# Five norms ahead of projections: one product with equal weights, a square root on ScalarE, a reciprocal on VectorE

## The reference

```python
def rms_norm(x, g):      # first block
    y = xf * lax.rsqrt(jnp.mean(xf * xf, axis=-1, keepdims=True) + EPS)
    return y * g

def layer_norm(x, g, b): # second block
    var = jnp.mean(jnp.square(xf - mu), -1, keepdims=True)
    return (xf - mu) * lax.rsqrt(var + LN_EPS) * g + b

# first block
proj = rms_norm(x, g_mix_pre) @ w_in          # place A
...
x = x + rms_norm(y, g_mix_post)
h = rms_norm(x, g_ffn_pre)                     # place B
x = x + rms_norm(conv_ffn(h, w_up, ..., w_down), g_ffn_post)
...
# second block, layers 0 and 1
x = layer_norm(ALPHA * x + y, ln_mix_g, ln_mix_b)                     # C (layer 0), E (layer 1)
x = layer_norm(ALPHA * x + swiglu(x, w_gate, w_up, w_down), ...)      # D (layer 0), read by od_w_in
```

## Time and profile before

| | |
|---|---|
| median of 3 runs | 914.29 us (914.2 to 915.26) |
| profiled execution | 914.49 us |
| its span in the profile | 912.7 us |
| PE busy | 890.2 us, 98% |
| PE weight loads | 843.1 us, 92% |
| DVE busy | 675.0 us, 74% |
| ACT busy | 507.9 us, 56% |
| POOL busy | 121.6 us, 13% |
| mean granted TensorE clock | 0.996 |

### The profile page before, as it was taken

One profiled execution on the slowest core, in us unless ns is written; L12 is line 12 of the kernel. 1 busy time (PEld: TensorE's weight loads), 2 busy tenths in 40 slices (PEclk: granted clock), 3 DMA queues, 4 the chain that ended last, 5 costly groups with the idle time before them and its releaser, 6 DMA issues.

```text
span 912.7 us, 18172 instructions
## 1 busy us (share of the span) xinstructions
PE 890.2 (98%) x6780; PEld 843.1 (92%) x6780; DVE 675.0 (74%) x1113; ACT 507.9 (56%) x750; POOL 121.6 (13%) x78
## 2 busy tenths in 40 slices
PE   5999899999999999999999999999999999999997
PEld 5977899999999999889999999999889999999996
DVE  5975797777777866788766686788767887668665
ACT  6345644334335645967555555566387765555552
POOL 1000000000000023002133230300130023324003
PEclk9999999999999999999999999999999999999999
DMA  8853275555564655445655655543334475555531
GB/s 311 324 212 116 70 225 189 184 188 179 184 196 151 198 193 163 139 140 161 208 173 174 198 175 178 164 128 126 116 117 139 126 229 187 173 195 176 180 139 46
DMA packets 44147, 156.76 MB, mean 172 GB/s; under 512 B 5082, under 2 KB 5573, under 8 KB 43973
## 3 DMA queue, kind: packets, MB, share of 16 engines
q1 hardware_dynamic: 42336, 152.17, 51.1%
q10 hardware_dynamic: 1317, 2.36, 0.7%
q0 software_dynamic: 448, 1.59, 0.5%
HBM read 155.04 MB, written 1.06 MB: 171 GB/s over the span
## 4 chain that ended last, share of the span: by engine, by line
PE 91%; ACT 3%; DVE 3%; issue 1%; DMA 1%; POOL 0%; SPq 0%; DVEq 0%; POOLq 0%
PE ps L399 21%; PE ps L400 21%; PE ps L401 21%; PE ps L444 5%; PE ps L446 5%; PE ps L445 5%; PE ps L416 2%; PE ps L423 1%; PE ps L417 1%; PE ps L793 1%; PE ps L504 1%; PE ps L506 1%; PE ps L505 1%; PE ps L528 1%; PE ps L814 1%
## 5 line engine op out<-in xcount | busy, mean ns | idle before, releaser
L399 PE MATMUL ps<-op_hi,w_hi 128*128 128x258 f32 (+1 forms) x1322 | 375.2, 284 | 1.6 <-DVE op_lo L1482 1.6
L401 PE MATMUL ps<-op_hi,w_lo 128*128 128x258 f32 (+1 forms) x1322 | 372.7, 282 | 0.0
L400 PE MATMUL ps<-op_lo,w_hi 128*128 128x258 f32 (+1 forms) x1322 | 372.4, 282 | 0.0
L1329 DVE TENSOR_TENSOR w_lo<-raw,w_hi 128x1024 fp32r<-128x1024 f32 x224 | 289.2, 1317 | 22.2 <-ACT w_hi L977 19.5
L977 ACT ACTIVATE w_hi<-raw 128x1024 fp32r<-128x1024 f32 x224 | 231.6, 1053 | 75.3 <-PE ps L401 41.7
L399 PEld LDWEIGHTS ps<-op_hi,w_hi 128*128 128x128 f32 x1322 | 249.6, 189 | 5.0 <-ACT bias L1289 2.0
L400 PEld LDWEIGHTS ps<-op_lo,w_hi 128*128 128x128 f32 x1322 | 250.4, 189 | 2.0
L401 PEld LDWEIGHTS ps<-op_hi,w_lo 128*128 128x128 f32 x1322 | 249.4, 189 | 0.0
L972 ACT ACTIVATE w_hi<-raw 128x1024 fp32r<-128x1024 f32 x60 | 63.5, 1058 | 61.7 <-PE ps L401 31.3
L399 PE MATMUL ps<-mix_hi,w_hi 128*128 128x256 f32 x336 | 96.0, 286 | 0.0
L400 PE MATMUL ps<-mix_lo,w_hi 128*128 128x256 f32 x336 | 94.6, 281 | 0.0
(11 more groups left out here) (278 smaller groups left out, 1081.8 us busy)
## 6 DMA issues: line engine op xcount, KB each, us to landing
raw<-in_stream SPq DMA_DIRECT2D x284, 512.0 KB, 3.6
x<-in_x SPq DMA_DIRECT2D x4, 256.0 KB, 5.7
bias<-bias_rows POOLq DMA_DIRECT2D x1, 1024.0 KB, 8.0
work<-in_last_norm SPq DMA_DIRECT2D x1, 1024.0 KB, 5.6
result<-y SPq DMA_DIRECT2D x4, 256.0 KB, 2.0
spans<-in_spans ACTq DMA_DIRECT2D x1, 576.0 KB
bias<-bias_rows POOLq DMA_DIRECT2D x1, 512.0 KB, 10.7
proj<-in_gmask ACTq DMA_DIRECT2D x1, 512.0 KB
```

The lines of the kernel that those rows point to most:

```text
L399: pe.matmul(o, wh, xh, start=start, stop=False, **kw)
L400: pe.matmul(o, wh, xl, start=False, stop=False, **kw)
L401: return pe.matmul(o, wl, xh, start=False, stop=stop, **kw)
L1329: m = dve.tensor_tensor(w_lo[:, s, :], raw[:, s, :], fp(w_hi[:, s, :]), ALU.subtract)
```

## The change

The mean square is now computed so that it comes out on all partitions at once, as a row of 256 tokens: one matmul with the 128 x 128 tile of 1/1024 as weights and the summed squares as the moving operand. ACT takes the square root from PSUM, with eps as its bias, and DVE the reciprocal.

- `sum_squares` adds down to one chunk: two additions of 512 columns as before, a third of 512, one of 256. PE's only wait is for the last.
- `square_mean` is one matmul of 256 columns. In the three networks it stands behind the first half of the third hidden unit's product, where it stood ahead of it.
- `spread` at A to E, the eps addition and POOL's power there are gone, and with them DVE's wait for POOL ahead of `split_lo`. POOL's list of statistics falls from seven to three (one at A, two elsewhere in the last layer).
- ACT gets `load_root` behind the squares (a Sqrt of one column that is used for nothing, so that the table set is loaded there), and `take_root` behind the next `split_hi`. At A, `load_root` first waits for two small memsets of POOL.
- DVE: `invert_root` (a `reciprocal` of 256 columns) in place of `copy_rinv`. At D it stands ahead of the `step()` that it followed.
- At A and B, PE computes the mean by token as well, from the one summed chunk (two matmuls of one column, four in the profile). At B, DVE makes `tok_ffn` from it right behind the reciprocal, ahead of the first hidden chunk; before it stood behind it.

The core of the diff:

```diff
-        STATISTICS = (2, 2, 2, 2, 4, 8, 2)
+        STATISTICS = (2, 4, 8)
...
             def square_mean(b):
-                def src(c):
-                    if c % 4 == 0:
-                        sums[0] += 1
-                        pe.wait_ge(S["sq_summed"], sums[0])
-                    return sq[:, c, :]
-                token_means(b, [(0, 0, [lambda c=c: src(c) for c in (0, 1, 4)])])
+                sums[0] += 1
+                pe.wait_ge(S["sq_summed"], sums[0])
+                pe.matmul(chunk(b, 0), mean_w[:, 0, :], sq[:, 0, :], start=True, stop=True, skip_group_check=True
+                          ).then_inc(S["square_mean_done"], 1)
...
                 first_chunks(bank(4, 0, n), bank(5, 0, n), operand, hi, lo)
+                out_chunk(bank(6, 0, n), hi, lo, half=0)
                 pe.wait_ge(S[free[0]], free[1])
                 square_mean(0)
-                out_chunk(bank(6, 0, n), hi, lo, half=0)
-                spread([(0, 0, SEQ), (1, 0, SEQ + P)])
+                if not shifted:
+                    token_means(1, [(0, 0, [sq[:, 0, :]])])
                 out_chunk(bank(6, 0, n), hi, lo, half=1)
...
                 if c == 0:
                     pe.wait_ge(S["pool_const"], 4)
                     square_mean(6)
+                    token_means(5, [(0, 0, [sq[:, 0, :]])])
                     pe.wait_ge(S["consts_loaded"], 16 * len(consts))
                     pe.matmul(ps[0:HEADS, 7, 0:384], rel[:], strip, start=True, stop=True
                               ).then_inc(S["table_ready"], 1)
-                if c == 2:
-                    spread([(0, 6, SEQ), (1, 6, SEQ + P)])
...
                 if c == 2:
-                    out_chunk(bank(2, 0, SEQ + 2), *raw_operand, half=0)
-                    spread([(0, 6, SEQ), (1, 6, SEQ + P)])
-                    out_chunk(bank(2, 0, SEQ + 2), *raw_operand, half=1)
+                    out_chunk(bank(2, 0, SEQ + 2), *raw_operand)
...
+            def load_root():
+                act.activation(root_warm[:], eps_col[:, 0:1], ACT.Sqrt)
+
+            def take_root(b, eps):
+                roots[0] += 1
+                act.wait_ge(S["square_mean_done"], roots[0])
+                act.activation(rinv[:, SEQ:512], chunk(b, 0), ACT.Sqrt, bias=eps_col[:, eps:eps + 1]
+                               ).then_inc(S["std_ready"], 1)
...
                     for part in range(2):
                         step(ahead=not (late and isinstance(j, int) and j == NFF - 1))
+                        if part == 0 and isinstance(j, int) and j == 0:
+                            take_root(0, 0 if convolve else 1)
...
-                m = dve.tensor_tensor(pair(sq, i), pair(sq, i), pair(sq, i + 1), ALU.add)
+                own.done(dve.tensor_tensor(pair(sq, i), pair(sq, i), pair(sq, i + 1), ALU.add))
                 if half:
-                    chained(m)
-                    m = dve.tensor_tensor(sq[:, 4, :], sq[:, 4, :], sq[:, 5, :], ALU.add)
-                m.then_inc(S["sq_summed"], 1)
+                    own.settle()
+                    chained(dve.tensor_tensor(pair(sq, 0), pair(sq, 0), pair(sq, 2), ALU.add))
+                    dve.tensor_tensor(sq[:, 0, :], sq[:, 0, :], sq[:, 1, :], ALU.add).then_inc(S["sq_summed"], 1)
...
-            def copy_rinv(b):
+            def invert_root():
                 rinvs[0] += 1
-                dve.wait_ge(S["spread_done"], stats.n)
-                dve.tensor_copy(rinv[:, 0:SEQ], chunk(b, 1)).then_inc(S["rinv_copied"], 1)
+                dve.wait_ge(S["std_ready"], rinvs[0] + 1)
+                dve.reciprocal(rinv[:, 0:SEQ], rinv[:, SEQ:512]).then_inc(S["rinv_copied"], 1)
                 dve.wait_ge(S["rinv_copied"], rinvs[0])
...
                     if begins:
-                        eps = RMS_EPS if convolve else LN_EPS
-                        hand_statistic(0, eps)
-                        dve.wait_ge(S["tok_rinv_ready"], stats.n)
                         step()
-                        copy_rinv(0)
+                        invert_root()
+                        if convolve:
+                            dve.wait_ge(S["stat_done"], 2)
+                            dve.tensor_scalar(tok_ffn[:], bank(1, 0, 2), RMS_EPS, RMS_EPS, ALU.add, ALU.mult)
...
                 if c == 0:
-                    hand_statistic(6, LN_EPS)
-                    dve.wait_ge(S["tok_rinv_ready"], stats.n)
-                step()
-                if c == 0:
-                    copy_rinv(6)
+                    invert_root()
+                step()
```

More of the change, by code:

```diff
@@ L136, in build @@
         minus_half = sb("minus_half", [P, 8])
+        eps_col = sb("eps_col", [P, 2])
+        root_warm = sb("root_warm", [P, 1])
         bias = sb("bias", [P, HEADS, 384])
@@ L192, in build @@
             split_hi_done split_done units_done sq_ready sq_summed mean_done
-            stat_done var_ready tok_rinv_ready spread_done x_ready norm_hi operand_ready z_ready centred evac
+            stat_done square_mean_done std_ready var_ready tok_rinv_ready spread_done x_ready norm_hi operand_ready z_ready centred evac
             row_sq_ready row_var_ready alpha_ready last_loaded row_root_ready rows_dve rows_act rows_turned
@@ L311, in _ @@
             pool.memset(minus_half[:], -0.5).then_inc(S["pool_const"], 1)
+            pool.memset(eps_col[:, 0:1], RMS_EPS).then_inc(S["pool_const"], 1)
+            pool.memset(eps_col[:, 1:2], LN_EPS).then_inc(S["pool_const"], 1)
             pool.memset(pad_b[:, :, 0:16], 0.0).then_inc(S["pool_const"], 1)
@@ L362, in _ @@
             row_roots(0)
-            inverse_root(1)
             row_roots(1)
@@ L371, in _ @@
             pool.memset(faded[0], 0.0).then_inc(S["faded_cleared"], 1)
-            inverse_root(3)
             norms[0] += 1
-            inverse_root(4)
+            inverse_root(1)
             pool.wait_ge(S["vop_lo"], 4)
             centre_x(3)
-            inverse_root(5)
-            inverse_root(6)
+            inverse_root(2)
             normed_x("ln_mix_g", "ln_mix_b", 1, 4, 2 * NFF)
@@ L549, in spread @@
                 m.then_inc(S["spread_done"], 1)
-            spreads = [0]
+            spreads = [1]
             def add_residual():
@@ L1032, in operand_hi @@
                         squares(i, pair(src, i))
+                    load_root()
                 seen[ready] += 4
@@ L1163, in _ @@
                 squares(i, pair(x, i))
+            act.wait_ge(S["pool_const"], 6)
+            load_root()
             for c in range(16):
                 step()
+                if c == 0:
+                    take_root(6, 0)
                 if c == 6:
@@ L1173, in moba_values_ready @@
                 act.wait_ge(S["units_done"], v_units)
+                act.wait_ge(S["tok_rinv_ready"], 1)
                 for t in range(2):
@@ L1224, in _ @@
                 step()
+                if c == 0:
+                    take_root(6, 1)
                 if c == 3:
@@ L1369, in hand_statistic @@
                 stats.n += 1
-                dve.wait_ge(S["stat_done"], stats.n)
+                dve.wait_ge(S["stat_done"], stats.n + (stats.n > 1))
                 if stats.n > 1:
@@ L1624, in hidden_chunk @@
                         split_lo()
-                        if convolve:
-                            dve.wait_ge(S["var_ready"], stats.n)
-                            own.done(dve.tensor_scalar(tok_ffn[:], tok_var[:, 0:2], eps, None, ALU.mult))
                 hidden_chunk(0, 0)
@@ L1674, in _ @@
                 if c == 0:
-                    hand_statistic(6, RMS_EPS)
+                    hand_statistic(5, RMS_EPS)
                     dve.wait_ge(S["table_ready"], 1)
@@ L1678, in _ @@
                                     ).then_inc(S["table_copied"], 1)
-                    dve.wait_ge(S["spread_done"], 1)
-                    chained(dve.tensor_copy(rinv[:, 0:SEQ], chunk(6, 1)))
+                    dve.wait_ge(S["std_ready"], 1)
+                    chained(dve.reciprocal(rinv[:, 0:SEQ], rinv[:, SEQ:512]))
                 if 4 <= c < 8:
@@ L1693, in _ @@
                     dve.wait_ge(S["evac"], EV_IN + 4)
+                    dve.wait_ge(S["pool_const"], 9)
                     n = 16 + SEQ
@@ L1852, in _ @@
             faded_pair(7)
-            dve.wait_ge(S["spread_done"], stats.n)
+            dve.wait_ge(S["spread_done"], stats.n - 1)
             dve.tensor_copy(rinv[:], bank(1)).then_inc(S["rinv_ready"], 1)
```

2 lines of the change are left out of this document (1 added, 1 removed).

## The result

The changed kernel takes 917.53 us (median of 10 runs, 915.97 to 921.25) against 914.42 for the kernel before in the same series (10 runs, 914.08 to 915.46). The ratio is 1.0036, with an interval of 1.0027 to 1.0045: slower by 3.1 us. The profiled execution took 919.06, its span 917.3, its mean granted clock 0.993.

The account below looks back on a forecast made before the run. The prediction took PE's queue to bound the kernel (busy for 98% of the span). With a reciprocal of 1.9, 0.4 + 0.8 + 0.5 + 0.4 + 0.5 = +2.6 on 914.29 gave 916.9 us, range 911.8 to 919.2.

Parts of the forecast that it names:

- A: First statistic, near 17 to 19 us: the table product waits for the one sum, 0.85 later less the spread's 0.44; 0.4 lost.
- D: Statistic ahead of L841, near 605 to 610 us: PE 0.4 later with a reciprocal of 1.9, 1.05 earlier with 0.42.
- B: Statistic ahead of L444, near 105 to 114 us, Gelu following: PE 0.8 later with a reciprocal of 1.9, 0.7 earlier with 0.42.
- the five places: The five statistics, A to E, each read by itself: together +2.6 us with a reciprocal of 1.9, -2.35 with 0.42.
- The reciprocal: DVE's new 256-column reciprocal: 1.9 us, from 7 ns an element in the four-column row; the sum is nought at about 1.26.
- The other bound, the copy: Lower bound for DVE's wide reciprocal: the 0.42 us of the 256-column copy that it replaces.
- its rival: At the five places, the reciprocal costs what a copy does: 911.9 us, faster; chance 0.23.
- C and E: Statistics ahead of Silu, the first near 412 to 420 us: PE 0.5 later at each with 1.9, 0.5 earlier with 0.42.
- the dear reciprocal: DVE's 256-column reciprocal at its forecast price of 1.9 us, against 0.42 for the cheap one.
- The third addition: DVE's extra addition, at B to D and the repeat of C: ends ahead of PE's need, so costed at nothing.
- The clock: Rival: the new waits lower TensorE's clock, 1.7 us a fall; 918.6 for one, 920.3 for two; chance 0.25.
- the forecast case: At the five places, a reciprocal of 1.9 and no fall of the clock: 916.9 us, by itself 915.5 to 917.8; chance 0.42.

## Why the prediction came out right

The direction, the time (916.9 forecast, 917.5 measured, in the range) and the cause hold; the way to the number was partly another one. It was forecast as +2.6 from the five places and no fall of the clock. The median rose by 3.1, of which the places gave 1.45; the other 1.65 is for the most part the clock (about 1.4 by the runs at 0.999).

- **The reciprocal.** Right, and it decided: 1.75 against 1.9, by its row of four columns. The other bound, the copy, was tried itself and gave a faster kernel, as its rival said (913.0; 911.9 forecast). The Trainium skill ("VectorE: DVE Perf Modes", section "Walkthrough: the 8-slice pipeline in each mode") tells of a divide with a repeat count of 8. The trace agrees with the prediction's reading of it, a cost paid for each element (6.25 ns); the page has no duration for it.
- **A: mis-sized, +0.4 against +0.60.** The one sum and the idle time came as worked out (PE at 18.29, forecast 18.25). The rest is that the term took the table product of before from the sum 17.02 + 1.23 and not from its own row (18.19), and that the mean and the four one-column products took 0.94 up to it, not 0.84.
- **B: +0.8 against +0.40.** The scaling was forecast at 110.56, which is 112.65 with the 2.09 of offset, and came at 112.28. 0.15 is the reciprocal; 0.12 is `tok_ffn`, put at 0.2, of which only 0.08 shows, since the scaling starts before the record of `tok_ffn` ends.
- **C and E: +0.5 against +0.20 and +0.21.** The scaling at C was forecast at 418.13 + 2.50 = 420.63 and came at 420.30: again 0.15 of the reciprocal, and the rest in the hand-overs, where DVE's next record starts up to 0.08 before the last one ends. Silu wasn't the limit, which the forecast said for the dear reciprocal too. What the forecast didn't see is how far the load of the Sqrt set already carried this term: without the load ahead of the split the idle times there are 0.5 (two experiments). It had counted the load as hidden behind POOL's wait, and so it was, measured against before; but that wait was a gain to be had.
- **D: +0.4 against +0.04.** Reciprocal at 609.03 for 609.15, `split_lo` at 610.81 for 611.05, the scaling at 611.96 for 612.35. The same small items add up, and each of them counts here in full. The third addition, put at nothing because it "ends ahead of PE's need", had a price here: it puts off a split of DVE by 0.70, PE waits 0.24 for that `w_lo`, and PE was ready for L837 at 611.86, which is 609.1 on the clock of before, not 608.7. It cost nothing only because DVE was later still.
- **Idle times of PE.** Forecast 1.9 at B, 1.7 at C and E, 2.1 at D, 1.2 at A; measured 1.45, 1.44, 1.44, 1.34, 0.94. A is shorter by the 0.3 that PE came later to it (L423 in front of it began at 15.28 instead of 14.96). "PE's waits higher by 8" was 6; "busy time lower by about 5" was 1.2, since it took work at full clock.
- **The clock: the step that failed.** "The granted clock behind B to E at 1.00" is wrong at D, and the prediction asked only about the waits of 1.7 and more, not about the 1.2 that it forecast at A. The row it argued from was an idle time of 2.34, and a fall was given a chance of a quarter. In fact 0.94 at A and 1.34 at D were followed by the lower level, and the 1.45 at B and 1.44 at C and E weren't (granted 1.00 over 112 to 124, 418 to 440 and 726 to 750). The price of one was nearly right at these places (1.7 put, 1.5 by the offsets), but not where it was read: ahead of B the 1.7 us of lost clock cost 0.6 us of time, since PE would have waited for ACT anyway. And of the 3.7 us that the prediction took from the mean clock, 1.5 lie behind PE's last product (granted 0.92 over 908 to 910 and 0.50 from there on), where they cost nothing. As a rival it gave 918.6 for one fall and 920.3 for two; the ten runs reach from 915.97, near the places' own cost, to 921.25, and the median lies between the forecast case and the rival. The prediction's number hit in part by luck: two errors, 1.15 too much at the places and 1.65 too little for the clock and the rest, had opposite signs and nearly cancelled.
- **Table loads.** The drain of 1.38 us that the Trainium skill ("ScalarE: Activation LUTs", section "What ACT_TABLE_LOAD costs") puts on every switch doesn't show in this case's traces: in the changed kernel, at C, the warm-up starts at 414.85, 0.01 after its load ends, and the load itself starts 0.02 after the squares end (412.40 + 1.14 to 413.56).

## What to carry to other kernels

Ask of a rewritten norm not how much work it takes from the busiest engine but which operation now stands alone between two of its stages. Here some 5 us of small products (a forecast, 5.4) were saved and given back because one 1.75 us reciprocal on 128 x 256 took the place of a copy and of POOL's small power, at places where PE's spare work was already used up; the same norm with the inverse root in one activation gave the gain. And count an idle time of the busiest engine of about a microsecond as a risk to its clock, even when work saved elsewhere pays for the time itself: here 0.94 of idle time was followed by 1.5 more of loss. It is a risk and no rule, since 1.45 in the same execution cost nothing more. Work that is there anyway, moved into the gap, left no fall at A in the three kernels that had it. And price a fall by what PE would have done at full clock: where it would have waited for somebody anyway, the fall cost 0.6 in place of 1.5.

## What the runs showed of the hardware that wasn't expected

- RECIPROCAL in fp32 on VectorE costs 6.25 ns an element of each partition (174 ns for 4 columns, 1749 for 256); the copy of the same tile within SBUF took 0.29 us, so the reciprocal is six times that.
- Abs_reciprocal_sqrt on ScalarE, from PSUM and with a bias pointer, took 0.46 us for 128 x 256, as long as Sqrt (0.47).
- TensorE's clock fell for 3.4 us behind idle times of 0.94 and 1.34 us in one execution, and not behind 1.45 in the same one; behind the 2.3 ahead of B it fell in seven of ten profiled executions, and behind 1.3 at D in three of four; behind the 3.1 at D and the 3.2 at E of the doubled reciprocal it stayed down for 6.9 (8 us at 0.57).
- A fall of the clock to 1.2 GHz for 3.4 us cost 1.5 us of time behind A and D, and 0.6 ahead of B, where PE would have waited 0.9 for ACT at full clock. For one and the same program a mean clock of 0.991 instead of 0.999 went with 5.3 us more time.
